# Gather transfers of 32 tokens and four picks, token rows laid out four times; weighted sums contracted over picks on four column strips of the array

## The reference

```
def block(args):
    xt, it, gt = args
    act = jax.nn.gelu(jnp.einsum('td,tkd->tk', xt, peer_u[it]), approximate=False)
    return jnp.einsum('tk,tkd->td', gt * act, peer_v[it])
```

## Time and profile before

| | us |
|---|---|
| median of 3 runs | 2608.28 |
| span of the profiled execution | 2607.3 |
| PE busy (8090 products) | 2152.8 |
| VectorE busy | 1647.3 |
| ScalarE busy | 1003.4 |
| GpSimd busy | 702.4 |
| mean rate of all transfers | 262 GB/s |

### The profile page before, as it was taken

How to read it: one execution, slowest core, us unless ns; L and a number is a source line. 1 busy time by engine, 2 the same in 40 slices (tenths; PEclk the granted TensorE clock), 3 DMA queues, 4 the chain that set the end, 5 groups by cost and what they waited for, 6 DMA issues and landing times. The chain is left out here.

```text
span 2607.3 us, 25567 instructions
## 1 busy us (share of the span) xinstructions
PE 2152.8 (83%) x8090; PEld 1334.7 (51%) x8090; DVE 1647.3 (63%) x3381; ACT 1003.4 (38%) x2477; POOL 702.4 (27%) x610
## 2 busy tenths in 40 slices
PE   6999978897878687877868887676777787899998
PEld 6778855676423232322324453232333474788877
DVE  5674266535888988878456776656766555555534
ACT  3213345323443343333334344435533455433322
POOL 0120031000444354443434454444444100000000
PEclk8999988998999899898989999787988897999999
DMA  7664200211899999999999999999999433222222
GB/s 243 218 208 113 67 5 26 77 61 75 340 419 420 400 403 420 396 420 398 415 380 415 414 414 411 420 370 359 420 419 420 159 92 122 91 97 97 80 81 97
DMA packets 142827, 683.18 MB, mean 262 GB/s; under 512 B 19648, under 2 KB 36320, under 8 KB 74224
## 3 DMA queue, kind: packets, MB, share of 16 engines
q0 software_dynamic: 73728, 536.90, 50.3%
q1 hardware_dynamic: 68976, 144.78, 17.0%
HBM read 679.50 MB, written 2.10 MB: 261 GB/s over the span
## 5 line engine op out<-in xcount | busy, mean ns | idle before, releaser
L2483 PE MATMUL peer_Y<-peer_w,peer_diag 128*128 128x512 f32 x1784 | 902.5, 645 | 242.2 <-ACT peer_diag L2469 215.2
L2428 POOL DMA_INDIRECT peer_w<-in_peer_uv,peer_eidx x510 | 606.4, 1189 | 703.7 <-PE peer_Y L2483 465.8
L2437 DVE CUSTOM_DVE_ANT_0 peer_w<-peer_w,peer_xtok 128x1024 f32<-128x1024 f32 x510 | 617.7, 1222 | 198.1 <-DMA peer_w<-in_peer_uv,peer_eidx 195.3
L2483 PEld LDWEIGHTS peer_Y<-peer_w,peer_diag 128*128 128x128 f32 x1784 | 337.8, 202 | 753.2 <-ACT peer_diag L2469 443.7
L2461 ACT ACTIVATE peer_gel<-peer_dots 128x1 f32<-128x1 f32 x512 | 103.8, 203 | 721.8 <-DVE peer_dots L2437 721.5
L2469 ACT ACTIVATE peer_diag<-all_ident,peer_a 128x128 f32<-128x128 f32 x448 | 179.8, 401 | 18.1 <-PE peer_Y L2483 3.6
L2463 ACT ACTIVATE peer_a<-peer_gel,peer_gates 128x1 f32<-128x1 f32 x512 | 150.8, 294 | 16.6
L2992 PE MATMUL m_acc<-m2x_hs,m2x_cut 128*128 128x512 f32 (+1 forms) x384 | 143.7, 374 | 6.4 <-PEq L123 3.7
L2993 PE MATMUL m_acc<-m2x_hs,m2x_cut 128*128 128x512 f32 (+1 forms) x384 | 143.3, 373 | 0.0
L2994 PE MATMUL m_acc<-m2x_hs,m2x_cut 128*128 128x512 f32 (+1 forms) x384 | 143.2, 373 | 0.0
L1293 ACT ACTIVATE p_cut<-m1h_raw 128x512 fp32r<-128x512 f32 (+2 forms) x96 | 58.2, 609 | 202.1 <-PE p_acc L1240 119.3
(11 more groups left out here) (518 smaller groups left out, 3731.2 us busy)
## 6 DMA issues: line engine op xcount, KB each, us to landing
m_gates<-in_w_ada SPq DMA_DIRECT2D x48, 512.0 KB, 4.3
m2x_raw<-in_w_up SPq DMA_DIRECT2D x22, 1024.0 KB, 4.8
m1h_raw<-in_w_in SPq DMA_DIRECT2D x80, 256.0 KB, 3.1
m20h_raw<-in_w_in SPq DMA_DIRECT2D x48, 256.0 KB, 7.3
m22h_raw<-in_w_in SPq DMA_DIRECT2D x48, 256.0 KB, 2.8
m_down_ring<-in_w_down SPq DMA_DIRECT2D x22, 512.0 KB, 3.4
m_out_ring<-in_w_out SPq DMA_DIRECT2D x16, 512.0 KB, 7.8
peer_w<-in_peer_uv,peer_eidx POOLq DMA_INDIRECT x510, 16.7
```

The lines of the kernel that those rows point to most:

```text
L2428: pool.indirect_dma_start(self.slot(n).rearrange("p c n -> p (c n)"), None, self.uv_dram, bass.IndirectOffsetOnAxis(self.col(self.eidx, n) ...
L2437: dve.tensor_tensor_reduce(u, u, self.xtok[:, n // PICKS, :], 1.0, 0.0, ALU.mult, ALU.add, self.col(self.dots, n)).then_inc(self.dotted, 1)
L2483: ins = pe.matmul(self.Y[:, h, :], self.diag[:, i % self.RD, :], self.slot(n)[:, 1, h * BANK:(h + 1) * BANK], start=(k == 0), stop=(i == l ...
```

## The change

The layout of a transfer is turned. Where a transfer brought one pick of 128 tokens, it now brings four picks of 32 tokens: partition 32c + i holds pick 4m + c of token 32q + i, for transfer q of batch m. The count, the rows and the bytes of the gather are the same. For the dot product, x must lie in the same way: the normed rows are stored to DRAM (`x_normed`) by `norm_rows`, and for each group of 32 tokens they are loaded four times over (`load_rows`, `xrep`), 16 loads of 512 KB in all. Those of tile 0 are issued by SyncE in `norm_rows`, the later ones by ScalarE in the last four steps of the tile before. TopK's last stage writes `eidx` and `gates` in the turned layout with 32 operations in place of 2.

Gelu, weight and weight matrix are made once per batch of four transfers: ScalarE makes gelu of four columns, VectorE the weights `a` and the four matrices `Z` of 128 x 32. PE then has eight products per batch (two halves, four strips): each contracts over 128 partitions and writes 32 partitions of `Y`. The fold on VectorE, the diagonal and the counts that went with them are gone. All four slots of a batch are free when its last product is done. `xtok` gives way to `xrep` and a `space` of two rows; `project` beside the gather has `raw` of four and `cut` of three.

```diff
@@ shape_constants @@
+    out["c_strips"] = np.tile(np.eye(32, dtype=np.float32), (4, 1))
...
@@ def norm_rows @@
-            load_early(sp, early_landed, early)
+            if out is None:
+                load_early(sp, early_landed, early)
+            else:
+                issue_early(sp, early_landed, early)
+                for t in range(NT):
+                    sp.wait_ge(scaled, t + 1)
+                    sp.dma_start(out[t * P:(t + 1) * P, :], xn[:, t % 2, :]).then_inc(stored[t % 2], 16)
+                for r in range(2):
+                    sp.wait_ge(stored[r], 16 * (NT // 2))
+                for q in range(4):
+                    gather.load_rows(sp, 0, q)
+                await_early(sp, early_landed, early)
...
+                if i >= 2 and out is not None:
+                    dve.wait_ge(stored[i % 2], 16 * (i // 2))
...
@@ def project @@
-    CUT = 4
+    CUT = 3 if side.BANKS else 4
...
@@ class TopK, vector, last stage @@
-            dve.scalar_tensor_tensor(self.eidx[:, t, ks], e[:, 0, ks], float(NKEYS), e[:, 1, ks], ALU.mult, ALU.add)
-            ins = dve.tensor_tensor(self.gates[:, t, ks].rearrange("p (h k) -> p h k", h=n), self.ex[:, hs], bc(self.rden[:, hs], 2, K), ALU.mult)
+            for q in range(4):
+                rows = slice(32 * q, 32 * q + 32)
+                for c in range(4):
+                    at, own = slice(32 * c, 32 * c + 32), slice(h0 * K + c, (h0 + n) * K, 4)
+                    items = slice(h0 * K + q, (h0 + n) * K, 4)
+                    dve.scalar_tensor_tensor(self.eidx[at, t, items], e[rows, 0, own], float(NKEYS), e[rows, 1, own], ALU.mult, ALU.add)
+                    ins = dve.tensor_tensor(self.gates[at, t, items].rearrange("p (h k) -> p h k", h=n), self.ex[rows, hs, c:K:4],
+                                            bc(self.rden[rows, hs], 2, K // 4), ALU.mult)
...
@@ class Gather @@
-    RW, RD = 9, 4
+    RW = 9
-    FOLDED = range(2 * PICKS, NT * PICKS)
-    SHARE = 4
+    BATCH = 4
...
+        self.xrep = ph.sb("xrep", [P, self.BATCH, D])
...
+        self.Z = ph.sb("Z", [P, 2, self.BATCH, 32])
...
+    def load_rows(self, engine, t, q):
+        rows = self.x_dram[t * P + 32 * q:t * P + 32 * q + 32, :]
+        engine.dma_start(self.xrep[:, q, :], bc(rows, 0, 4)).then_inc(self.x_landed[q], 16)
...
@@ fetch @@
-                pool.wait_ge(*self.consumed(n - self.RW))
+                pool.wait_ge(self.used, (n - self.RW) // self.BATCH + 1)
...
@@ vector @@
+        m = s // self.BATCH - 1
+        if s % self.BATCH == 0 and 0 <= m < self.N // self.BATCH:
+            t, k = divmod(m * self.BATCH, PICKS)
+            dve.wait_ge(self.gelued, m + 1)
+            dve.tensor_tensor(self.a[:, m % 2, :], self.gel[:, m % 2, :], self.gates[:, t, k:k + self.BATCH], ALU.mult).then_inc(self.weighed, 1)
+            dve.wait_ge(self.weighed, m + 1)
+            if m >= 2:
+                dve.wait_ge(self.used, m - 1)
+            dve.tensor_tensor(self.Z[:, m % 2], bc(self.strips[:], 1, self.BATCH), bc(self.a[:, m % 2, :], 2, 32), ALU.mult).then_inc(self.spread, 1)
...
+            if n % PICKS < self.BATCH:
+                dve.wait_ge(self.x_landed[q], 16 * (t + 1))
...
-        if 0 <= n < self.N and not self.on_pe(n):
...
-            y = self.resid[:, n // PICKS, :]
-            dve.scalar_tensor_tensor(y, self.slot(n)[:, 1, :], self.col(self.a, n), y, ALU.mult, ALU.add).then_inc(self.folded, 1)
...
@@ scalar @@
-        act.wait_ge(self.dotted, n + 1)
-        act.activation(self.col(self.gel, n), self.col(self.dots, n), ACT.Gelu).then_inc(self.gelued, 1)
...
+        if k >= PICKS - self.BATCH and t + 1 < NT:
+            act.wait_ge(self.dotted, n + 1)
+            self.load_rows(act, t + 1, n % self.BATCH)
+        if n % self.BATCH == self.BATCH - 1:
+            m = n // self.BATCH
+            act.wait_ge(self.dotted, n + 1)
...
+            act.activation(self.gel[:, m % 2, :], self.dots[:, m % 2, :], ACT.Gelu).then_inc(self.gelued, 1)
@@ tensor @@
...
+        pe.wait_ge(self.spread, m + 1)
...
+        for q in range(self.BATCH):
+            pe.wait_ge(*self.landing(first + q))
         for h in range(2):
-            ins = pe.matmul(self.Y[:, h, :], self.diag[:, i % self.RD, :], self.slot(n)[:, 1, h * BANK:(h + 1) * BANK],
-                            start=(k == 0), stop=(i == last))
+            for q in range(self.BATCH):
+                ins = pe.matmul(self.Y[32 * q:32 * q + 32, h, :], self.Z[:, m % 2, q, :], self.slot(first + q)[:, 1, h * BANK:(h + 1) * BANK],
+                                start=(k == 0), stop=(k == PICKS - self.BATCH))
         ins.then_inc(self.used, 1)
...
@@ peer_and_front @@
-        xtok = ph.sb("xtok", [P, NT, D])
+        x_dram = nc.dram_tensor("x_normed", (SEQ, D), F32).ap()
...
+        space = ph.sb("space", [P, 2, D])
...
@@ second_front @@
-                ring = Early(ph3.sb("raw", [P, 6 if pacer is not None else KD, BANK], side="right"), project_loads([(d["w_in_2"][:, 3 * 512 + GLA_RANK:4 * 512 + GLA_RANK], None)]))
+                ring = Early(ph3.sb("raw", [P, 4 if pacer is not None else KD, BANK], side="right"), project_loads([(d["w_in_2"][:, 3 * 512 + GLA_RANK:4 * 512 + GLA_RANK], None)]))
```

More of the change, by code:

```diff
@@ L238, in load_early, with issue_early, await_early @@
 def load_early(sp, sem, early):
[L240 to L244, removed]
+    issue_early(sp, sem, early)
+    await_early(sp, sem, early)
+def issue_early(sp, sem, early):
+    for e in early:
+        for dst, src in e.loads:
+            sp.dma_start(dst, src).then_inc(sem, 16)
+def await_early(sp, sem, early):
+    n = sum(len(e.loads) for e in early)
+    if n:
+        sp.wait_ge(sem, 16 * n)
 class Side:
@@ L650, in _, with norm_rows @@
             side.tensor(pe, len(tiles) - 1)
-def norm_rows(nc, name, consts, resid, hs, gain_dram, meta=None, load=None, early=(), keep=None, stats=None):
+def norm_rows(nc, name, consts, resid, hs, gain_dram, meta=None, load=None, early=(), stats=None, out=None, gather=None):
     ident, half = consts["ident"], consts["half"]
@@ L2395, in landing @@
         return (self.lent_landed[n], 16) if n < E else (self.landed[(n - E) % self.RW], 16 * ((n - E) // self.RW + 1))
-    def on_pe(self, n):
-        return n not in self.FOLDED or n % self.SHARE != self.SHARE - 1
-    def products(self, n):
-        return sum(1 for m in range(n) if self.on_pe(m))
-    def consumed(self, n):
-        return (self.used, self.products(n + 1)) if self.on_pe(n) else (self.folded, n + 1 - self.products(n + 1))
-    @staticmethod
-    def col(x, n):
-        return x[:, n // PICKS % x.shape[1], n % PICKS:n % PICKS + 1]
+    def load_rows(self, engine, t, q):
+        rows = self.x_dram[t * P + 32 * q:t * P + 32 * q + 32, :]
+        engine.dma_start(self.xrep[:, q, :], bc(rows, 0, 4)).then_inc(self.x_landed[q], 16)
     def fetch_first(self, pool):
@@ L2415, in fetch_to @@
     def fetch_to(self, pool, step):
-        self.fetch(pool, min(self.N, step + self.RW - 3))
+        limit = self.fetched
+        while limit < self.N and (limit < self.RW + len(self.lent) or (limit - self.RW) // self.BATCH * self.BATCH + self.BATCH < step):
+            limit += 1
+        self.fetch(pool, limit)
     def fetch(self, pool, limit):
@@ L2616, in peer_and_front @@
                 xs = ph2.line("xs", [P, 2, KD, SEQ])
-                norm_rows(nc, "n2", consts, resid, xs, d["g_ffn_row"], early=[ring, tables], keep=xtok, stats=stats)
+                norm_rows(nc, "n2", consts, resid, xs, d["g_ffn_row"], early=[ring, tables], stats=stats, out=x_dram, gather=gather)
                 Phase.gathering = True
@@ L2621, in peer_and_front @@
             gather.open()
-            pick(nc, gather, top, qT, tables["keys"], mod, kept.rows, STANDALONE)
+            pick(nc, gather, consts["ident"], top, qT, tables["keys"], mod, kept.rows, STANDALONE)
         pacer = Pacer(gather, STANDALONE)
-        second_front(nc, consts, resid, mod, d, kept, HALF, xtok[:, 0:2, :], qT[:].rearrange("p h q -> p (h q)"), pacer)
+        space = ph.sb("space", [P, 2, D])
+        second_front(nc, consts, resid, mod, d, kept, HALF, space[:], qT[:].rearrange("p h q -> p (h q)"), pacer)
         finish_gather(nc, gather, pacer.next)
```

71 lines of the change are left out of this document (29 added, 42 removed).

## The result

| | median us | range us | span of the profiled execution us |
|---|---|---|---|
| before (same chip, beside it) | 2608.65 | 2608.04 to 2618.59 | |
| after | 2803.56 | 2797.08 to 2810.28 | 2806.7 |

The ratio is 1.0738 with an interval of 1.0709 to 1.0768: the change costs 195 us. Forecast were 87, with a range that ended at 2800.

The account below looks back on a forecast made before the run. The gather's DMA transfers, near 420 GB/s, were taken to bound the kernel, so engine savings were worth nothing. Terms 15 + 6 + 8 + 3 + 28 + 15 + 12 = 87 us gave 2695 us, own range 2640 to 2745, whole range 2622 to 2800.

Parts of the forecast that it names:

- 12 row loads, bytes and tile ends: Row loads within the gather: 15 us for 6.3 MB at 420 GB/s, plus 6 us (0 to 20) at three tile ends.
- TopK's last stage, start and tails: 32 operations for 2, 3.2 us more per call: +3 us before the first fetch, +3 at each tail; calls 1 to 3 covered.
- norm_rows: Before peer_query: stores and the third scale's wait for the first store delay the start by 8 us (bounds 0 and 12).
- release by four, all gaps: In the gather: slots freed by fours cut least slack from 13.2 to 3.7 us, so TopK tails, long and shorter gaps cost more.
- the smaller rings of `project`: Beside the gather: raw ring of 4 (from 6) and cut ring of 3 (from 4) cost 0.
- the three TopK tails: Ends of TopK calls on VectorE: 9.3 us more each, 28 us together, including 3 each for the longer last stage.
- the two long gaps: Gaps without a dot before 1342 and 1777 us: 7.5 us more each, 15 us together.
- elsewhere: Shorter gaps of 4 to 10 us in front of HALF, about 30: about 0.4 us each, 12 us (0 to 50).
- PE: A batch's products on four strips: 7.3/3 = 2.4 us at full clock (bounds 1.8 and 7.3), 4.8 at the lower clock.
- Rival B: PE strips run one after another, or as good as: 7.3 us a batch, 154 us lost, about 2820 us; chance 0.15.
- D: Rival, faster: holes are PE's catching up and all 33 us come back, 2601 or 2593 us; chance 0.10.
- C: Rival, cover is enough: gaps cost nothing more, only loads and start add 26 us, 2634 us; chance 0.14.

Follow-up runs that it names:

- no loads: The kernel after without the 12 loads of token rows at tile ends, all tiles using tile 0's rows: 2692.83 us, ratio 1.0314.
- plain rows: The kernel after with each row load as one 512 KB DMA of the tile's 128 consecutive rows, no repeat: 2701.33 us, ratio 1.0352.
- two repeats: The kernel after with each row load as two DMAs of 64 partitions, source of 32 rows repeated twice: 2863.96 us, ratio 1.0979.
- with the wait gone: The kernel after with four buffers instead of two for the normed tiles in norm_rows: 2797.39 us, ratio 1.0731.
- the three costs taken out: The kernel after without tile-end row loads, with TopK's last stage in 2 instructions and four normed-tile buffers: 2658.95 us, ratio 1.0199.
- the obvious repair: The kernel after with row loads as four DMAs of 32 partitions, all issued behind the tile's last gelu: 2753.08 us, ratio 1.0556.
- loads by 32: The kernel after with each row load cut into four DMAs of 32 partitions, same queue and place: 2725.65 us, ratio 1.0464.

## Why the prediction was wrong

The direction and the bound held, and the holes at the TopK tails deepened. The sum did not: 87 us against 195. Taken apart by the runs (each difference is good to some 5 us):

| term | forecast us | measured us | by |
|---|---|---|---|
| 12 row loads, bytes and tile ends | 15 + 6 | 111 | after less no loads, 2803.56 - 2692.83 |
| of it, what plain rows would cost | 21 | 8.5 | 2701.33 - 2692.83 |
| TopK's last stage, start and tails | 3 + 9 | 31 | 2803.56 - 2772.14 |
| norm_rows | 8 | 10.3 | 2.9 + 7.4, by first fetches |
| release by four, all gaps | 19 + 15 + 12 | 45 | a remainder: 2658.95 - 2606.93, less 7.4 |
| sum | 87 | 197 | measured whole: 195 |

**Tile ends, the step that failed.** The prediction took a row load for one like those of the earlier trace rows, landing within the 10 us until its own dot, and gave three tile ends 6 us (0 to 20). The rows it took the price from were loads whose outer dimension is 128 partitions; that of bc(rows, 0, 4) is the 4 of the repeat. The trace has it at a share of 0.26 and 105 GB/s, with two repeats 0.13 and 52; with plain rows beside the gather the rate stayed near 420. At 105 GB/s, 4 x 0.524 MB take 20 us, all in one queue with ScalarE's gelu behind them. VectorE waited 62.0 us for rows, and a tile end lost 36 to 42. The Trainium skill ("DMA: Bandwidth & Descriptors", "Rules for kernel authors") says just this: a leading zero-stride broadcast of c copies confines a DMA to at most c engines. With that rule the trace agrees, for c of 4 (0.26) and of 2 (0.13), and the prediction should have weighed it against the row loads. It weighed a rule for PE, where nothing came of it, and none for the DMA that the diff adds. With plain rows even the 15 us of bytes was more than the 8.5 us measured.

**TopK's last stage, a size that was off.** 0.105 us each was read from a single pair with other work behind it. In a row of 32 a pair takes 0.33 us from start to start (936.75 to 937.08) and all of them 5.5 us, and calls 1 to 3, forecast as covered, are not: windows 720 to 740 and 800 to 820 dip to 325 and 327 GB/s, and with two operations they move 386 and 401. 31 us against 12.

**norm_rows**: 8 forecast, 10.3 measured, though by another way. The prediction made the third scale's wait for its store the main part; with the wait gone 2.9 us came back, and 7.4 are left with SyncE's wait for its stores and the issue of its loads ahead of the next stage. No run without the stores tests that.

**Release by four, right in size, not in its parts.** 46 forecast, 45 left. But the 45 is a remainder, in which the strips, the matrices `Z` and the smaller rings of `project` (forecast 0) stand too; none of these was taken out alone. By windows of 10 us over the gather, what is missing to 420 GB/s grows from 47 us before to 89 with the other costs taken out, the same 42 as the gather's length. At the three TopK tails it grows by 21 (forecast 19), at the two long gaps by nothing (forecast 15), and elsewhere by 20 (forecast 12). So the right sum is in part luck.

That release by four cost 82 us in the kernel before was not foreseen. One cost that the prediction doesn't have is in both kernels. HeadNorm's root is made by GpSimd, whose queue is in order, and with grouped release it stands behind four transfers that all wait for one group of slots. VectorE waits for that root, and the dots of the next groups stand behind that wait. VectorE's waits for it in `project`: before, before with release by four, and with the three costs taken out:

```profile
DVE peer_xtok L815 <- POOL m20i_rstd L821: 1.9, 2, 1.6
...
DVE peer_xtok L815 <- POOL m20i_rstd L821: 19.3, 4, 6.4
...
DVE peer_space L839 <- POOL m20i_rstd L845: 21.8, 4, 6.9
```

The rate there is 414 GB/s before (1465 to 1520), 278 with release by four (1510 to 1580, 24 us missing) and 349 with the three costs out (1518 to 1578, 10 missing). How much of that is this wait no run tells by itself. Why the second loses more is argued, not shown: there each of a group's last picks still needs its own chain over ScalarE, its own four records on PE (1.8 us, by the earlier trace rows), or a fold on VectorE.

**PE.** Forecast 2.4 us a batch at full clock and 4.8 at the lower one. Measured 3.41 at a granted clock of 0.54 (window 1407 to 1411), which at full clock would be near 1.8 (an estimate), the bound for all four at once. Rival B is refuted: in the steady stretch of 120 us the rate is 421 GB/s. The weight loads of a batch lie in that time too, 16 at three moments 0.85 us apart (8, 4 and 4), while products run. So the Trainium skill's rule on row groups ("TensorE: Matmul & The Clock Gate", Part 3), of which the prediction was wary, cost nothing that can be seen here, though all strips use all rows.

**D and C.** D falls: the tails became deeper, from 13.5 to 46 us. C falls too: with loads, last stage and the norm buffers' wait taken out, 52 us remain, of which 45 aren't the start.

## What to carry to other kernels

Read the access pattern of every DMA that a change adds, its outermost dimension first: the repeat of a broadcast put there costs more than the bytes, and holds what is queued behind it on the issuing engine. Where a ring of buffers feeds a saturated queue, price a coarser release by what else stands in the consumer's queue between the first and the last of a group (a norm waiting for its gain, a TopK tail), and look what stands behind the grouped transfers in the issuer's queue, for the consumer may wait for it. When freeing the queue from one thing delays another with a single buffer, try both orders: here the obvious repair cost 27 us.

## What had not been expected of the hardware

- A DMA from ScalarE's queue whose source of 32 rows is repeated four times moves 105 GB/s at a share of 0.26; repeated twice, 52 GB/s at 0.13, however many are queued. Eight such issues span 41.70 us on ScalarE, of which 34 lie behind the last dot.
- Loads of 32 partitions and 128 KB, 16 in a row beside the gather, kept the share at 1.0 but brought the rate down to 271 to 302 GB/s over 28 us (loads by 32, 1392 to 1420), while beside plain loads of 512 KB it stayed at 411 to 424 (plain rows, 1020 to 1040 and 1380 to 1404). Why was not tried.
- Four products side by side on strips of 32 columns, with all 128 rows in use, took 3.41 us for 16 records at a granted clock of 0.54. In a row they would take 16 x 0.46 / 0.54 = 13.6 us, scaled from nine full ones, an estimate: a factor 4.
- Operations on 32x32 elements stand 0.17 us apart on VectorE in the mean (5.5 us for 32), those on 32x8 in the calls of two heads 0.13 us (4.2 us for 32).
